# Second expert table: 64 of 256 tokens taken by gathered rows instead of the dense product

## The chip, the cores and the metric

The kernel runs on one core of one Trainium2 chip. The metric is the device time in microseconds of one execution; the value compared is the median of several runs. The engines are TensorE (PE), VectorE (DVE), ScalarE (ACT), GpSimd (POOL) and SyncE (SP), each with an instruction queue of its own.

## The reference, cut to what matters

The program is a first block of two layers (two feed-forward parts around a mixer) and a second block of two layers, each a mixer and an expert part `_peer`. The change touches only the expert part, which runs twice. It has 16384 experts; each of the 256 tokens chooses 128 of them (8 heads of 16), with a softmax gate for each:

```python
    eidx = jnp.take_along_axis(cidx, pos, axis=-1).reshape(T, PEER_HK)
    gate = jax.nn.softmax(sc.astype(jnp.float32), axis=-1).astype(x.dtype).reshape(T, PEER_HK)
...
        ub = jnp.take(u_tab, ib, axis=0)
        act = jax.nn.gelu(jnp.einsum('td,tkd->tk', xb, ub), approximate=False)
        vb = jnp.take(v_tab, ib, axis=0)
        return jnp.einsum('tk,tkd->td', gb * act, vb)
```

The width d is 1024 and everything is float32.

## The kernel before, in words

The expert part does not gather. It computes the activations of all 16384 experts for all 256 tokens, multiplies them by a matrix of gates that is zero where an expert wasn't chosen, and multiplies the result by the whole second table. Both tables come from `in_stream`, 512 KB at a time ("a unit", 128 experts x 1024), through `ring` (three slots, SP's `load`, L497) and are split into two fp32r parts, high and low, in `wsp` (three slots): ACT writes the high part (L454), DVE the low part (L457). A product of two split numbers takes three matmuls, high x high, high x low and low x high (`PARTS`).

**First table (stages U and U2, 92 and 36 units).** Each unit gives 24 matmuls (L721) and one activation. Of each unit's 256 tokens, the columns of the second 128 are written to DRAM (`second_dram`, L518 and L521, SP), to be transposed into the layout that the second table's stage reads. Meanwhile the gates of the first 128 tokens reach the same DRAM tensor by 128 indirect DMAs with addition on POOL (L688, semaphore `scattered`), each of 128 elements. The gates of the second 128 tokens are built in U2 from one-hot matrices in groups of four tokens (`GROUPS` = 32, one group behind each unit from the 94th on): DVE builds four one-hot tiles (L2645, L2654), PE multiplies (L1342, eight matmuls a group), ACT moves them (L1807).

**Second table (stage V, 128 units).** For each unit j: SP fetches `back[j % 4]` from `second_dram` (L527) after waiting for `gated`; DVE multiplies the unit's slice of `arena` by it (`gate`, L2671); ACT writes the high part of the result to `hsp` (`stage`, L1789), DVE the low part (`low`, L2676); PE runs `value_unit` (L1349), which is `down_unit` (L778): two blocks of 128 tokens, each three parts by two halves of 512 columns, 12 matmuls 128x512 (L785), summed over all 128 units in four PSUM banks `ACC`. DVE's order for a unit is gate(j+1), low(j), split of the next unit; ACT's is stage(j), split. The order on each engine is as the code is written; the engines are held together by semaphores alone. POOL has nothing to do in V but fetch `h` and two rows for the layer norm after unit 40 (`RESTORE_AT`, L694). SP issues in V, for each unit, one load of 512 KB and one `back` of 128 KB. After the last unit, DVE adds the four banks to `h` (`add_block`, L1908) and the layer norm follows.

## Time and profile before

| | us |
|---|---|
| median of 3 runs | 2987.77 (2987.75 to 2992.1) |
| the profiled execution | 2988.89 |
| its span in the trace | 2986.9 |
| PE busy in it | 2928.5 |
| DVE busy | 2124.6 |
| ACT busy | 1498.2 |
| POOL busy | 680.0 |

Busy times are sums of instruction durations. Matmuls overlap one another in the pipeline, so their spacing is read from start times. A row of the timeline has the start, the duration, the engine, the line of the kernel, the operation, what it writes and reads, the shape and the count; in square brackets stands the idle time of the engine just before, and what ended it. Stages are told apart by their lines: U2 has L1342, V has L785 with `hsp` and `wsp`.

### The profile page before, as it was taken

Reading aid. Unit: us, or ns where it says so; the run is one execution under the profiler, and the core shown is the slowest. Engines: PE = TensorE matmul, PEld = TensorE weight load, DVE = VectorE, ACT = ScalarE, POOL = GpSimd, SP = SyncE. Lnnn points to the kernel's source line nnn. Section 1 sums busy time; section 2 is a strip of 40 time slices with the busy share of each in tenths; the row PEclk is TensorE's granted clock in tenths of the full one; section 3 lists DMA queues with packets and bytes.
Section 4 is the critical chain, followed back from the end, with each engine's and each line's share of the span. In section 5 each row is a group of like instructions: output and inputs, shape, how many; then the busy total and the mean of one; then the engine's idle time right before and its main releaser. Section 6 shows DMA issues by size and latency. Waiting matters only on the chain.

```text
span 2986.9 us, 54746 instructions
## 1 busy us (share of the span) xinstructions
PE 2928.5 (98%) x18452; PEld 2598.6 (87%) x18452; DVE 2124.6 (71%) x3656; ACT 1498.2 (50%) x2410; POOL 680.0 (23%) x443
## 2 busy tenths in 40 slices
PE   8999999999999999999999999999999999999998
PEld 7888888888878888899999988888899999988887
DVE  6667566766766667758986677777758996767776
...
GB/s 222 190 161 180 153 167 186 174 183 189 148 233 113 184 187 152 157 173 199 198 211 189 176 247 262 243 240 203 163 163 191 196 209 197 176 235 266 239 244 189
DMA packets 255982, 581.52 MB, mean 195 GB/s; under 512 B 61336, under 2 KB 127168, under 8 KB 255344
## 3 DMA queue, kind: packets, MB, share of 16 engines
...
HBM read 542.92 MB, written 36.84 MB: 194 GB/s over the span
## 4 chain that ended last, share of the span: by engine, by line
PE 81%; DVE 10%; ACT 4%; issue 2%; DMA 2%; POOL 1%; SPq 0%; DVEq 0%; ACTq 0%
PE acc L785 31%; PE work L721 26%; PE work L731 9%; PE work L733 5%; DVE wsp L457 4%; PE acc L1205 2%; PE acc L849 2%; ACT wsp L454 2%; DMA ring<-in_stream 2%; PE acc L1342 1%; ACT scratch L1421 1%; PE work L1127 0%; POOL st L584 0%; DVE scratch L2033 0%; PE work L1242 0%
## 5 line engine op out<-in xcount | busy, mean ns | idle before, releaser
L457 DVE TENSOR_TENSOR wsp<-ring,wsp 128x1024 fp32r<-128x1024 f32 x908 | 1105.2, 1225 | 568.7 <-ACT wsp L454 564.4
L454 ACT ACTIVATE wsp<-ring 128x1024 fp32r<-128x1024 f32 x944 | 984.9, 1052 | 506.1 <-PE work L721 251.8
L721 PE MATMUL work<-xsp,wsp 128*128 128x256 f32 x7872 | 971.7, 285 | 6.2 <-DVE wsp L457 3.2
L721 PEld LDWEIGHTS work<-xsp,wsp 128*128 128x128 f32 x7872 | 953.8, 192 | 11.2 <-DVE wsp L457 4.5
L785 PE MATMUL acc<-wsp,hsp 128*128 128x512 f32 x4128 | 955.4, 390 | 6.6 <-DVE hsp L2676 4.7
L785 PEld LDWEIGHTS acc<-wsp,hsp 128*128 128x128 f32 x4128 | 767.8, 188 | 171.1 <-issue 4.4
L731 PE MATMUL work<-xsp,wsp 128*128 128x512 f32 x1408 | 503.7, 400 | 6.5 <-DVE xsp L1861 5.0
L688 POOL DMA_INDIRECT second_dram<-rows_sb,spots x256 | 465.8, 1819 | 148.4 <-issue 90.8
L733 PE MATMUL work<-xsp,wsp 128*128 128x256 f32 x1408 | 395.8, 281 | 0.0
L731 PEld LDWEIGHTS work<-xsp,wsp 128*128 128x128 f32 x1408 | 265.4, 188 | 74.6 <-DVE xsp L1861 6.1
L584 POOL TENSOR_TENSOR st<-st,mhalf 128x1 f32<-128x1 f32 x24 | 20.6, 862 | 1356.4 <-DVE st L1881 805.0
L1789 ACT ACTIVATE hsp<-arena 128x256 fp32r (+1 forms) x256 | 107.0, 418 | 336.4 <-PE acc L785 322.7
L733 PEld LDWEIGHTS work<-xsp,wsp 128*128 128x128 f32 x1408 | 266.7, 189 | 3.1
L2676 DVE TENSOR_TENSOR hsp<-arena,hsp 128x256 fp32r<-128x256 f32 x256 | 108.8, 425 | 60.1 <-ACT hsp L1789 60.0
L1456 ACT ACTIVATE hsp<-scratch 128x256 fp32r<-128x256 f32 x88 | 36.8, 418 | 218.4 <-DVE scratch L1954 218.4
L1448 ACT ACTIVATE scratch<-scratch 128x256 f32<-128x256 f32 x88 | 36.8, 418 | 188.1 <-DVE scratch L1944 188.1
L680 POOL TENSOR_TENSOR wsp<-ring,wsp 128x1024 fp32r<-128x1024 f32 x36 | 89.7, 2492 | 130.6 <-ACT wsp L454 130.4
L2671 DVE TENSOR_TENSOR arena<-arena,back 128x256 f32 (+1 forms) x256 | 107.2, 419 | 10.5 <-ACT arena L1807 6.0
L849 PE MATMUL acc<-wsp,xsp 128*128 128x512 f32 x384 | 100.8, 413 | 0.0
L1205 PE MATMUL acc<-wsp,xsp 128*128 128x512 f32 x384 | 93.9, 397 | 0.0
L849 PEld LDWEIGHTS acc<-wsp,xsp 128*128 128x128 f32 x384 | 72.9, 197 | 16.2
L1205 PEld LDWEIGHTS acc<-wsp,xsp 128*128 128x128 f32 x384 | 70.3, 188 | 15.3
...
## 6 DMA issues: line engine op xcount, KB each, us to landing
...
back<-second_dram SPq DMA_DIRECT2D x256, 128.0 KB, 3.2
...
second_dram<-rows_sb,spots POOLq DMA_INDIRECT x256
...
```

Of the source, the lines that this page charges most:

```text
L454: self.eng.activation(dst[:, 0, :], src, ACT.Copy).then_inc(high_done, 1)
L457: self.eng.tensor_tensor(dst[:, 1, :], src, dst[:, 0, :].bitcast(F32), ALU.subtract)\
L688: pool.indirect_dma_start(out=second_dram[l], in_=selv[:, 0, 2, n:n + 1], in_offset=None, out_offset=bass.IndirectOffsetOnAxis(spots[:, n: ...
L721: mm = pe.matmul(out_, lhsT=w[:, a, 128 * c:128 * c + 128], rhs=xsp[:, b, c, :], start=(c == 0 and n == 0), stop=(c == DC - 1 and n == 2))
L731: pe.matmul(out_, lhsT=w[:, 0, 128 * c:128 * c + 128], rhs=xcs[:, c, :, :].rearrange("p s t -> p (s t)"), start=(c == 0), stop=False)
L733: mm = pe.matmul(out_[:, 0:T], lhsT=w[:, 1, 128 * c:128 * c + 128], rhs=xsp[:, 0, c, :], start=False, stop=(c == DC - 1))
L785: mm = pe.matmul(ACC[2 * b + n][:, :], lhsT=act[:, pa, 128 * b:128 * b + 128], rhs=w[:, pw, 512 * n:512 * n + 512], start=(first and m == ...
L849: mm = pe.matmul(ACC[2 * (g % 2) + b][:, :], lhsT=xsp[:, px, c, 128 * b:128 * b + 128], rhs=w[:, pw, 512 * cc:512 * cc + 512], start=(c == ...
L1205: mm = pe.matmul(ACC[2 * (g % 2) + b][:, :], lhsT=xsp[:, px, c, 128 * b:128 * b + 128], rhs=w[:, pw, 512 * cc:512 * cc + 512], start=(c == ...
L1789: act.activation(hsp[:, j % 2, 0, :], arena[:, bass.ds(it * (6 * T) + j * T, T)], ACT.Copy)\
L2671: tt(a, a, back[j % 4], ALU.mult).then_inc(gated, 1)
L2676: tt(hsp[:, j % 2, 1, :], arena[:, bass.ds(it * (12 * T) + j * T, T)], hsp[:, j % 2, 0, :].bitcast(F32), ALU.subtract).then_inc(act_low, 1)
```

## The change

The second 128 tokens are split into 64 that stay dense (`KEPT`) and 64 that are gathered (`FETCHED`). `arena`, `gate`, `stage`, `low` and `back` shrink from 256 to 192 columns. `GROUPS` falls from 32 to 16.

On PE a value unit has 10 matmuls: the first 128 tokens as before (6), and the 64 kept tokens with their high and low parts interleaved as 128 columns of the stationary side (`gsp`), times the high and the low part of the weights by two halves (4). After the last unit ACT copies these two banks out (`packed`), and PE folds high and low rows together and adds the gathered rows' sum with four float32 matmuls against `fold` (L1485, L1486 of the new kernel).

The 64 gathered tokens have 128 chosen experts each, 8192 rows. They lie on 128 partitions, a token's first eight choices of a head on one, the other eight on the one 64 further. So POOL issues, per layer, 64 indirect DMAs that fetch 128 rows of 4 KB each (`fetch`, 512 KB) into seven slots of `fetched`, and 64 that fetch the 128 activations belonging to them (`fetch_act`, 4 bytes each) from `second_dram`. DVE multiplies activations by gates in four batches of 16 (`coefficients`). Of each seven rows, DVE adds four with one instruction each (`add_row`, 128x1024), and for three (`BY_POOL`) ACT scales the row in place (`scale_row`, 128x1024) and POOL adds it (128x1024). Seven rows are worked into each twelve units ("a round"), from unit 14 to unit 121; nine rounds, and one row more. A slot is fetched anew only when its row has been added, and POOL's queue holds, for each row, its own addition, the fetch for the row seven later, and one or two `fetch_act`. `fetch` for rows 0 to 6 stands before V; POOL then waits for the end of U2, clears the two totals, waits for the last activations to be in DRAM and issues 16 `fetch_act`; the first `coefficients` on DVE waits for those.

Small parts: before the last 16 scatters POOL waits for the second tokens' gates and issues three DMAs that move indices and gates of the upper choices to the lower 64 partitions; every first-table activation is now written in two pieces (L1799 and L1800 before did so in U2 alone), with the second in one of four `acts` slots that is reused once its DMA has landed; POOL's restoring of `h` stands after round 3. The three indirect forms have index lists made on the chip.

On PE, one value unit in the loop before (`wsp` and `hsp` are the split weights and activations):

```order
L1356 UNCONDITIONAL_BRANCH
L1356 ISA
L405 REGISTER_ALU
L785 MATMUL acc<-wsp,hsp 128x512 x12
L1351 REGISTER_ALU
```

and now (`gsp` holds the interleaved parts):

```order
L1475 ISA
L444 REGISTER_ALU
L1460 MATMUL acc<-wsp,gsp 128x512 x4
L1467 MATMUL acc<-wsp,gsp 128x512 x6
L1454 REGISTER_ALU
```

Twelve matmuls of 128x512 became ten, in two statements.

On DVE, inside the loop over the value units, before:

```order
L2669 REGISTER_ALU
L2671 ISA
L2671 TENSOR_TENSOR arena<-arena,back_81 128x256
L2675 REGISTER_ALU
L2676 TENSOR_TENSOR hsp<-arena,hsp 128x256
L456 REGISTER_ALU
L457 TENSOR_TENSOR wsp<-ring,wsp 128x1024
```

and now, from the second unit of a round:

```order
L2852 REGISTER_ALU
L2854 ISA
L2854 TENSOR_TENSOR arena<-arena,back_89 128x192
L2858 REGISTER_ALU
L2859 TENSOR_TENSOR gsp<-arena,gsp 128x192
L502 REGISTER_ALU
L503 TENSOR_TENSOR wsp<-ring,wsp 128x1024
L2736 ISA
L2739 ISA
L2739 SCALAR_TENSOR_TENSOR row_total<-fetched,coef,row_total 128x1024
```

The two short operations are 192 wide, and behind four of the twelve splits there is now an addition of a row, which waits for that row's DMA.

On POOL, from the scatters to the end of V, before (all of it):

```order
L676 COMPARE_AND_BRANCH
L688 DMA second_dram<-rows_sb,spots 4194304x1 x128
L694 DMA h<-h_saved_dram 128x2048
L614 DMA rows_sb<-in_rows 128x1024
L615 DMA rows_sb<-in_rows 128x1024
```

and now, its beginning up to the third row of the first round:

```order
L763 DMA second_dram<-rows_sb,spots 4194304x1 x112
L756 DMA gidx<-gidx 64x8x8 x2
L757 DMA fgate<-fgate 64x8x8
L763 DMA second_dram<-rows_sb,spots 4194304x1 x16
L742 DMA fetched<-in_stream,gidx 128x1024 x7
L770 MEMSET row_total 128x1024
L771 MEMSET row_total_62 128x1024
L748 DMA coef<-second_dram,gidx 128x1 x16
L742 DMA fetched<-in_stream,gidx 128x1024
L748 DMA coef<-second_dram,gidx 128x1 x2
L786 TENSOR_TENSOR row_total_62<-row_total_62,fetched 128x1024
```

After 128 scatters POOL had three DMAs; now there are 128 indirect DMAs and 28 additions, each in a queue whose next instruction waits for it.

The diff, cut:

```diff
-GROUPS = P // 4
+FETCHED = 64
+TD = T - FETCHED
+KEPT = TD - P
...
+HALF_K = TOPK // 2
+ROWS = PH * HALF_K
+SLOTS = 7
+ROUNDS = ROWS // SLOTS
+BY_POOL = (1, 3, 5)
+BATCH = 16
+BATCHES = ROWS // BATCH
+SEGMENTS = ((0, 2, 1), (2, 4, 2), (4, 6, 3), (6, 9, 4))
+ROW_AT = (1, 2, 4, 6, 7, 9, 11)
+USES = [len(range(s, ROWS, SLOTS)) for s in range(SLOTS)]
 ROUND = 16 * TOPK
...
+                sp.dma_start(second_rows[l][bass.ds(it * UNITS_BODY + j, 1)][:, :, P:T].rearrange("a p t -> p (a t)"),
+                             acts[:, j % 4, :]).then_inc(acts_slot[j % 4], 16)
...
+                sp.dma_start(back[j % 4][:, 0:TD], second_rows[l][bass.ds(it * UNITS_BODY + j, 1)][:, :, 0:TD].rearrange("a p t -> p (a t)"))\
                   .then_inc(back_in[j % 4], 16)
...
+                def fetch(m):
+                    r, k = m % SLOTS, place_of(m)
+                    if m >= SLOTS:
+                        if r in BY_POOL:
+                            pool.wait_ge(used_pool, by_pool(ROWS) * l + by_pool(m - SLOTS + 1))
+                        else:
+                            pool.wait_ge(used_dve, by_dve(ROWS) * l + by_dve(m - SLOTS + 1))
+                    pool.indirect_dma_start(out=fetched[:, r, :], out_offset=None, in_=value_rows,
+                                            in_offset=bass.IndirectOffsetOnAxis(gidx[:, 0, k:k + 1], 0))\
+                        .then_inc(row_in[r], 16)
+
+                def fetch_act(m):
+                    k = place_of(m)
+                    pool.indirect_dma_start(out=coef[:, m:m + 1], out_offset=None, in_=second_dram[l],
+                                            in_offset=bass.IndirectOffsetOnAxis(gidx[:, 1, k:k + 1], 0))\
+                        .then_inc(elem_in[m // BATCH], 16)
...
+                    if i == PH - 1:
+                        pool.wait_ge(ev("sel_ready"), 3 * (l + 1))
+                        for w in range(2):
+                            pool.dma_start(low_halves(gidx[0:64, w, :]), high_halves(gidx[64:P, w, :])).then_inc(rows_moved, 16)
+                        pool.dma_start(low_halves(fgate[0:64, :]), high_halves(fgate[64:P, :])).then_inc(gates_moved, 16)
...
+                pool.wait_ge(rows_moved, 32 * (l + 1))
+                for m in range(SLOTS):
+                    fetch(m)
+                pool.wait_ge(unit_done, Group(f"peer{l}", "V").u)
+                pool.memset(row_total, 0.0)
+                pool.memset(row_total2, 0.0).then_inc(totals_clear, 1)
                 for s in range(4):
...
+                    pool.wait_ge(acts_slot[s], 16 * SPILLS * (l + 1))
+                for m in range(BATCH):
+                    fetch_act(m)
+                more = BATCH
+                for t in range(ROUNDS):
+                    for r in range(SLOTS):
+                        m = SLOTS * t + r
+                        if r in BY_POOL:
+                            n = by_pool(ROWS) * l + by_pool(m)
+                            pool.wait_ge(row_scaled, n + 1)
+                            pool.wait_ge(totals_clear, l + 1)
+                            if n:
+                                pool.wait_ge(used_pool, n)
+                            pool.tensor_tensor(row_total2, row_total2, fetched[:, r, :], ALU.add).then_inc(used_pool, 1)
+                        if m + SLOTS < ROWS:
+                            fetch(m + SLOTS)
+                        while more < min(ROWS, BATCH + (4 * m + 6) // 3):
+                            fetch_act(more)
+                            more += 1
+                    if t == 3:
+                        pool.wait_ge(scattered, ROUND * PH * (l + 1))
+                        pool.wait_ge(g_done, GROUPS * (l + 1))
+                        pool.wait_ge(gated, NKEYS * l + RESTORE_AT)
+                        pool.dma_start(h, saved).then_inc(h_back, 16)
+                        load_rows(rows2[2 * l + 2, 0], rows2[2 * l + 2, 1])
+                pool.wait_ge(used_dve, by_dve(ROWS) * (l + 1))
+                pool.wait_ge(used_pool, by_pool(ROWS) * (l + 1))
+                pool.tensor_tensor(row_total, row_total, row_total2, ALU.add).then_inc(ev("rows_added"), 1)
                 serve(pool, moments[:, 0, 1:2])
                 serve(pool, moments[:, 1, 1:2])
...
-                    down_unit(G, i, hsp[:, i % 2, :, :], first, last, 6 * n)
+                    w = G.unit(pe, i, 6 * n)
+                    both = gsp[:, i % 2, :, :].rearrange("p t s -> p (t s)")
+                    act = gsp[:, i % 2, :, :]
+                    for m in range(2):
+                        for n in range(2):
+                            mm = pe.matmul(ACC[2 + n][:, :], lhsT=both[:, 2 * P:2 * TD], rhs=w[:, m, 512 * n:512 * n + 512],
+                                           start=(first and m == 0), stop=(last and m == 1))
+                    if last:
+                        mm.then_inc(ev("packed_done"), 1)
+                    order = [(m, n) for n in range(2) for m in range(3)] if last else [(m, n) for m in range(3) for n in range(2)]
+                    for m, n in order:
+                        pa, pw = PARTS[m]
+                        mm = pe.matmul(ACC[n][:, :], lhsT=act[:, 0:P, pa], rhs=w[:, pw, 512 * n:512 * n + 512],
+                                       start=(first and m == 0), stop=(last and m == 2))
+                        if last and m == 2 and n == 0:
+                            mm.then_inc(ev("half_block"), 1)
+                    mm.then_inc(unit_done, 1)
...
+                pe.wait_ge(ev("rows_added"), l + 1)
+                for n in range(2):
+                    pe.wait_ge(packed_out, 2 * l + n + 1)
+                    c = slice(512 * n, 512 * n + 512)
+                    pe.matmul(ACC[2 + n][:, :], lhsT=fold[:, 64:192], rhs=row_total[:, c], start=True, stop=False)
+                    mm = pe.matmul(ACC[2 + n][:, :], lhsT=fold[:, 0:P], rhs=packed[:, c], start=False, stop=True)
+                    mm.then_inc(ev("first_block" if n else "half_block"), 1)
...
+                    if q >= 4:
+                        act.wait_ge(acts_slot[q % 4], 16 * (SPILLS * l + q // 4) + (4 * UNITS_BODY) * it)
+                    act.activation(arena[:, bass.ds(it * (UNITS_BODY * TD) + q * TD, P)], G.bank(q)[:, 0:P], ACT.Gelu)
+                    G.free(act.activation(acts[:, q % 4, :], G.bank(q)[:, P:T], ACT.Gelu), q)
...
+                    act.activation(gsp[:, j % 2, :, 0], arena[:, bass.ds(it * (12 * TD) + j * TD, TD)], ACT.Copy)\
                        .then_inc(act_high, 1)
+
+                def scale_row(m, it=0):
+
+                    r = m % SLOTS
+                    act.wait_ge(row_in[r], 16 * (USES[r] * l + m // SLOTS + 1) + 16 * it)
+                    act.activation(fetched[:, r, :], fetched[:, r, :], ACT.Copy, scale=coef[:, bass.ds(it * SLOTS + m, 1)])\
+                       .then_inc(row_scaled, 1)
...
+                for first, last, batches in SEGMENTS:
+                    act.wait_ge(ev("coef_ready"), BATCHES * l + batches)
+                    with act.Fori(0, last - first) as it:
+                        for j in range(12):
+                            k = 14 + 12 * first + j
+                            stage(k, it)
+                            split.one(G.u + k + 1, it, 12)
+                            if j in ROW_AT and ROW_AT.index(j) in BY_POOL:
+                                scale_row(SLOTS * first + ROW_AT.index(j), it)
...
+                    m = slice(BATCH * b, BATCH * (b + 1))
+                    if b == 0:
+                        dve.wait_ge(gates_moved, 16 * (l + 1))
+                    dve.wait_ge(elem_in[b], 16 * BATCH * (l + 1))
+                    c = coef[:, m].rearrange("p (h k) -> p h k", k=HALF_K)
+                    heads = BATCH // HALF_K
+                    g = fgate.rearrange("p (h k) -> p h k", k=TOPK)[:, heads * b:heads * (b + 1), 0:HALF_K]
+                    step(tt(c, c, g, ALU.mult))
+                    dve.memset(st[:, 31:32], 0.0).then_inc(ev("coef_ready"), 1)
...
+                def add_row(m, it=0):
+
+                    r = m % SLOTS
+                    n = by_dve(ROWS) * l + by_dve(m)
+                    per_round = SLOTS - len(BY_POOL)
+                    dve.wait_ge(row_in[r], 16 * (USES[r] * l + m // SLOTS + 1) + 16 * it)
+                    if n:
+                        dve.wait_ge(used_dve, n + per_round * it)
+                    stt(row_total, fetched[:, r, :], coef[:, bass.ds(it * SLOTS + m, 1)], row_total, ALU.mult, ALU.add)\
+                        .then_inc(used_dve, 1)
...
+                    a = arena[:, bass.ds(it * (12 * TD) + j * TD, TD)]
+                    tt(a, a, back[j % 4][:, 0:TD], ALU.mult).then_inc(gated, 1)
...
+                    tt(gsp[:, j % 2, :, 1], arena[:, bass.ds(it * (12 * TD) + j * TD, TD)],
+                       gsp[:, j % 2, :, 0].bitcast(F32), ALU.subtract).then_inc(act_low, 1)
...
+                dve.wait_ge(totals_clear, l + 1)
+                for first, last, batches in SEGMENTS:
+                    coefficients(batches - 1)
+                    with dve.Fori(0, last - first) as it:
+                        for j in range(12):
+                            k = 14 + 12 * first + j
+                            gate(k + 1, it)
+                            low(k, it)
+                            split.one(V.u + k + 1, it, 12)
+                            if j in ROW_AT and ROW_AT.index(j) not in BY_POOL:
+                                add_row(SLOTS * first + ROW_AT.index(j), it)
                 split.next = V.u + 123
+                add_row(ROWS - 1)
```

## Rows read from the trace of the kernel before

**Rows 1.** Page, parts 1 and 5: busy time of PE; POOL's indirect scatter and its split.
```profile
PE 2928.5 (98%) x18452; PEld 2598.6 (87%) x18452; DVE 2124.6 (71%) x3656; ACT 1498.2 (50%) x2410; POOL 680.0 (23%) x443
...
L688 POOL DMA_INDIRECT second_dram<-rows_sb,spots x256 | 465.8, 1819 | 148.4 <-issue 90.8
...
L680 POOL TENSOR_TENSOR wsp<-ring,wsp 128x1024 fp32r<-128x1024 f32 x36 | 89.7, 2492 | 130.6 <-ACT wsp L454 130.4
```

**Rows 2.** Windows: stretch, length, busy by engine, clock, DMA share, GB/s; U2, then V.
```profile
1600.00:1710.00 110.00, 110.00 (x1035) 108.67 (x1033) 80.51 (x154) 61.34 (x131) 68.00 (x39) 1.00 0.75 181
1720.00:2060.00 340.00, 337.30 (x1485) 278.55 (x1486) 245.91 (x374) 170.37 (x249) 1.73 (x3) 1.00 0.75 246
```

**Rows 3.** Timeline of V, DVE rows of one unit (layer 1).
```profile
1802.30 1.23 DVE L457 TENSOR_TENSOR wsp<-ring,wsp 128x1024 fp32r<-128x1024 f32 x1 [0.52 <-ACT wsp L454]
1803.44 0.42 DVE L2671 TENSOR_TENSOR arena<-arena,back 128x256 f32 x1
...
1805.01 1.23 DVE L457 TENSOR_TENSOR wsp<-ring,wsp 128x1024 fp32r<-128x1024 f32 x1 [0.53 <-ACT wsp L454]
```

**Rows 4.** Timeline of PE: first and last matmuls around V; units of U2.
```profile
1714.19 2.00 PE L785 MATMUL acc<-wsp,hsp 128*128 128x512 f32 x8
...
2066.20 4.70 PE L743 MATMUL work<-xsp 128*128 128x512 f32 x20
...
2610.15 0.63 PE L1342 MATMUL acc<-one_hots 128*128 128x128 f16 x8
2610.59 3.12 PE L721 MATMUL work<-xsp,wsp 128*128 128x256 f32 x24
2613.55 0.63 PE L1342 MATMUL acc<-one_hots 128*128 128x128 f16 x8
...
2617.39 8.88 PE L721 MATMUL work<-xsp,wsp 128*128 128x256 f32 x72
2626.11 4.27 PE L785 MATMUL acc<-wsp,hsp 128*128 128x512 f32 x18
```

**Rows 5.** Line L688: duration ns min/median/max.
```profile
L688 POOL DMA_INDIRECT second_dram<-rows_sb,spots x256: 1537/1581/2631, 1390.3 to 2595.1; - x128
```

**Rows 6.** Timeline of POOL and DVE in U: scatters beside splits.
```profile
1577.69 2.58 POOL L688 DMA_INDIRECT second_dram<-rows_sb,spots  x1 [0.30 <-issue]
1580.57 2.58 POOL L688 DMA_INDIRECT second_dram<-rows_sb,spots  x1 [0.30 <-issue]
...
1577.62 1.23 DVE L457 TENSOR_TENSOR wsp<-ring,wsp 128x1024 fp32r<-128x1024 f32 x1 [1.66 <-ACT wsp L454]
```

**Rows 7.** Timeline of POOL and DVE in U: casts beside POOL's addition.
```profile
1355.53 2.40 POOL L680 TENSOR_TENSOR wsp<-ring,wsp 128x1024 fp32r<-128x1024 f32 x1 [0.47 <-ACT wsp L454]
...
1355.70 2.28 DVE L2519 CAST pfa<-posa 128x64 f16<-128x64 uint32 x1
1358.02 0.20 DVE L2520 CAST pfb<-posi 128x64 f16<-128x64 uint32 x1
```

**Rows 8.** Timeline, POOL and SP: a wait for scatters; the last scatter; SP's reads after it.
```profile
1653.08 2.21 POOL L688 DMA_INDIRECT second_dram<-rows_sb,spots  x1 [4.59 <-DMA second_dram<-rows_sb,spots]
...
1689.59 1.63 POOL L688 DMA_INDIRECT second_dram<-rows_sb,spots  x1 [0.30 <-issue]
...
1701.74 0.36 SPq L527 DMA_DIRECT2D back<-second_dram  x1
...
1718.28 0.80 SPq L527 DMA_DIRECT2D back<-second_dram  x2
```

**Rows 9.** Windows in V while h and two rows also came (columns as Rows 2).
```profile
1828.00:1832.00 4.00, 2.68 (x12) 1.88 (x10) 1.90 (x3) 1.60 (x3) 0.00 (x0) 1.00 0.91 360
2736.00:2740.00 4.00, 4.00 (x19) 3.30 (x19) 1.47 (x3) 0.62 (x2) 0.00 (x0) 1.00 1.00 361
```

**Rows 10.** Windows of the first mixer: PE idle, then the clock.
```profile
290.00:292.00 2.00, 0.11 (x1) 0.00 (x0) 0.80 (x1) 2.00 (x5) 2.00 (x4) 1.00 0.98 358
294.00:296.00 2.00, 2.00 (x16) 1.88 (x15) 0.83 (x3) 0.24 (x1) 0.00 (x0) 0.50 1.02 268
```

153 lines of the change are left out of this document (95 added, 58 removed).

## The prediction

> **What bounds the kernel now.** I read the page first: PE is busy 2928.5 us, 98% of the span [rows 1]. The windows then show it in both stages that the change touches: 110.00 of 110 us in U2, 337.30 of 340 in V, at full clock, while DVE is at 246 and ACT at 170 of those 340 and POOL does next to nothing [rows 2]. So in V the matmuls set the pace. From the start of one split to the next are 1805.01 - 1802.30 = 2.71 us [rows 3], 0.226 for each of 12 matmuls. V lasts 2066.20 - 1714.19 = 352 us a layer [rows 4], 128 units and 5 us of start. Everything here is made against the profiled execution, 2988.9 us with 2986.9 of span, 1.1 over the median.
>
> **What PE gains.** Ten matmuls in place of twelve are 2.26 us a unit, 128 x 2.26 = 289 us a layer. If nothing else changed, V would be 58 us shorter. In U2 a unit with a one-hot group takes 2613.55 - 2610.15 = 3.40 us, one without 8.72/3 = 2.91 (2617.39 to 2626.11) [rows 4]; sixteen groups less are 16 x 0.49 = 7.8 us a layer. PE is full there, so I count them whole. I price the stationary side read with a gap at nothing; double would make it the bound, and that is counted below.
>
> **What POOL must now do in V.** This is the term that decides. An indirect DMA holds POOL for 1.82 us on the mean of 256 and 0.30 passes before the next can start: 2.12 [rows 1, 6]. The smallest is 1.54 [rows 5], so 1.84. The large ones come from DVE: the scatter at 1577.69 starts 0.07 after a split and takes 2.58, which is what is left of the split (1.16) plus 1.42; the next one meets the next split and takes 2.58 again, 2.88 a turn [rows 6]. No trace here shows an indirect DMA that fetches 4 KB rows. Each issue handles 128 indices as the scatter does, so I take the scatters' 2.12, with 1.84 and 2.88 as ends. An addition of 128x1024 on POOL is 2.49 us [rows 1]; with its wait for DVE's port 2.75.
>
> The Trainium skill, SBUF — State Buffer (Who interferes with whom), says that a DVE instruction with two SBUF inputs and a GpSimd instruction that reads SBUF exclude one another for a whole instruction. The trace shows the lock in both directions: beside POOL's addition a cast of 0.20 us took 2.28, ending with it [rows 7], and the scatters above waited for the split. By that page all of DVE's V work contends.
>
> For a round of twelve units POOL has 7 fetches, 9.3 fetches of activations while these last, and three additions: 16.3 x 2.12 + 3 x 2.75 = 42.9 us. PE's twelve units take 27.1. For the time of PE a fetch would have to cost (27.1 - 8.25)/16.3 = 1.15 us, below anything the trace shows. **So POOL sets the pace** until the last activation has been asked for, behind row 35. Row m+7 can't be fetched before POOL comes by in its queue, and DVE, which has gate, low and split of the next units queued behind the row's addition, waits there; PE waits for DVE. Seven slots let DVE be one round ahead and no more.
>
> In order of time, from the first matmul of V:
> - 5 us: POOL clears two totals and waits for the last activations in DRAM; SP's reads behind the same wait went at 1718.28, 4.1 us after V's start [rows 4, 8]. In the first layer POOL comes from its row fetches: the last scatter was issued at 1691.2 [rows 8], the three copies (3 us) and 7 x 2.12 bring it to 1709, and V now starts at 1706; that hides in the 5.
> - 16 x 2.12 = 34 us for the first activations, 4 to land (a wait for scatters ended 4.59 us after the last [rows 8]), and 6 for DVE's two units and first addition: 49. DVE is there after 14 units, at 32 us, so PE stands for some 12 us.
> - Rows 0 to 35: 36 + 48 = 84 indirect DMAs, 178.1 us; 15 additions, 41.3; restoring h, three short issues, 2: 221. That is 270.
> - Row 42 lands and DVE takes up unit 86: 4 + 2, 276.
> - 42 units remain. POOL needs only 7 x 2.12 + 8.25 = 23 us a round now. But DVE has a round's 12 x (1.14 + 2 x 0.27) + 4 x 1.2 = 25 us (1803.44 - 1802.30 for a split, the gate's spacing less 64 columns [rows 3]), and the three additions of POOL can stop it for 3 x 2.3 more: 32. And the DMA engines: 524 + 98 KB a unit and 7/12 of 524 for rows are 928 KB, at 360 GB/s [rows 9] 2.57 us. Between PE's 2.26 and DVE's 2.66 I take 2.5 for 36 units and 2.26 for six: 104. That is 380.
> - The tail: two evictions and four float32 matmuls behind the last unit. Four matmuls at 0.226 would be 0.9, at four times that 3.6, since these are plain float32; I take 2.5, an estimate. POOL's last addition hides in the six last units.
>
> V is then 382, 30 more than before. The three copies ahead of the last 16 scatters push these back by about 3 us, while SP comes to them 7.8 us earlier; SP's first read stood 10.5 us behind the last scatter's end (1701.74 against 1691.2), so up to 3 us of waiting arise there: 1.5. Per layer 30 - 7.8 + 1.5 = 24, for two 47: 2988.9 + 47 = 3036, and I say **3035**.
>
> What costs nothing: the second activation of each U unit (ACT is busy 170 of 340 in V, and 61 of 110 in U2, where it already does two [rows 2]); the four index operations of DVE before V; the slots of `acts`, reused after four units, 11 us, against a landing of a few; ACT's three scalings a round, in an engine with half its time free.
>
> The Trainium skill, DMA: Bandwidth & Descriptors (Specifications), gives about 358 GB/s of HBM for a core; by it the late rounds would take 2.59 us a unit. The rows show the same figure.
>
> **Rivals.**
> - *POOL is cheaper.* Fetches run at 1.84 and DVE isn't held up: 5 + 29.4 + 10 for the start, 84 x 1.84 + 15 x 2.49 + 2 = 194, then 6 + 42 x 2.26 + 2.5 = 103: V is 342. With 7.8 and 1.5 that is 16 less a layer, 2956. With my other terms the kernel breaks even at V = 358, which is 170 + 100 x, x = 1.88 a fetch. That is near, and so the sign hangs on a quarter of a microsecond. For it: 1.58 is the median of the scatters [rows 5], and DVE, while it waits for rows, doesn't hold the port. Against: the mean was 1.82 with DVE no fuller than in the new V.
> - *The change gives all of PE's gain.* V is 289 + 7, and the sum 2 x (56 + 7.8) less: 2862. It needs fetches of 1.15 us.
> - *POOL is dearer*, by locking step with the splits at 2.88 as in [rows 6], or because a fetch of 4 KB rows costs more to describe. V = 170 + 288 = 458, 100 more a layer: 3189. Half way is 3110.
> - *The clock.* After PE had been busy 0.11 of 2 us, its granted clock was 0.50 (1.2 GHz instead of 2.4) for the next microseconds [rows 10]. While POOL sets the pace, a row takes 6.1 us and PE works 12/7 x 2.26 = 3.9 of it. At half clock this would be 7.7, above 6.1, and if it lasted for all 36 rows it would cost 58 us a layer: 3150. Since PE works two thirds of that time, I expect it for a part only, hidden in the waits. The gapped stationary side lies here too: at double load time (0.376 for each of ten) a unit is 3.8 us.
> - *It doesn't do what it says*: the order of the instructions shows ten matmuls and 16 groups, so only the tail could be other than said, by microseconds.
>
> **How the numbers follow.** The forecast (POOL sets the pace of five rounds, fetches between 1.95 and 2.35, late rounds between 2.26 and 2.66; 3000 to 3085) gets 0.47. The cheaper POOL, 2940 to 3000, 0.27; the whole gain 0.05; the dearer POOL and the clock 0.19; 0.02 for what I don't see. Leaving out the whole gain and the top of the dearer case, the range is 2945 to 3125. A measurement of this kernel tells 0.2%, 6 us, from no change. Of the cheaper case nine tenths lie below 2982: faster 0.30, same 0.07, slower 0.63.
>
> **What would show it.** In the profile of the changed kernel: POOL's two indirect forms back to back from V's start, with a mean near 1.8 us and 0.3 between; a PE stretch idle for some 10 us about 32 us into V; in the first two thirds of V, DVE's additions of rows waiting for DMAs whose issue waited in POOL's queue, PE busy about 65%, and DMA below 300 GB/s; then a last third with PE nearly full, a unit in 2.4 to 2.7 us and DMA near 350 GB/s; U2 8 us shorter. The forecast is wrong if fetches take 1.5 us or less between starts, if the rows' landings and not POOL's queue hold DVE, or if PE is the one that is full throughout V.

## The result and the profile after

The changed kernel took 3050.65 us (3038.73 to 3056.78, 4 runs) against 2988.16 (2987.75 to 2992.1, 4 runs) for the kernel before: a ratio of 1.0203, 95% interval 1.0178 to 1.0227. It is slower, by about 2%, inside the range and 16 us above the predicted 3035. The profiled execution of it was one of 3056.78 us, so its trace stands some 6 us above the median.

The page of the changed kernel, parts 1 and 5 (columns as in the rows of before):

```profile
span 3054.9 us, 53849 instructions
...
PE 2879.0 (94%) x17700; PEld 2517.0 (82%) x17700; DVE 2233.0 (73%) x3634; ACT 1539.7 (50%) x2616; POOL 1194.6 (39%) x765
...
L763 POOL DMA_INDIRECT second_dram<-rows_sb,spots x256 | 496.0, 1937 | 127.2 <-issue 80.7
...
L742 POOL DMA_INDIRECT fetched<-in_stream,gidx x128 | 183.5, 1434 | 157.0 <-DVE row_total L2739 132.1
...
L748 POOL DMA_INDIRECT coef<-second_dram,gidx x128 | 155.8, 1218 | 52.8 <-issue 38.4
...
L786 POOL TENSOR_TENSOR row_total<-row_total,fetched 128x1024 f32<-128x1024 f32 x54 | 132.6, 2456 | 55.7 <-ACT fetched L1929 55.1
```

PE has fallen from 98% busy [rows 1] to 94%: it is no longer full. The new rows say at once that the fetches are cheap. Their means of 1.43 and 1.22 us are below the 1.94 us of the scatters in the same trace, and in front of the row fetches POOL was idle for 132 us, waiting for DVE's additions.

The timeline of PE, from the end of U2 to the matmuls with `fold`, first layer 0, then layer 1. U2's matmuls are L824, a unit of V is L1460 and L1467, the matmuls with `fold` are L1485 and L1486:

```profile
1705.35 4.60 PE L824 MATMUL work<-xsp,wsp 128*128 128x256 f32 x24 [1.99 <-DVE wsp L503]
1709.79 1.09 PE L1460 MATMUL acc<-wsp,gsp 128*128 128x512 f32 x4
...
2086.35 1.08 PE L1460 MATMUL acc<-wsp,gsp 128*128 128x512 f32 x4
2087.26 1.56 PE L1467 MATMUL acc<-wsp,gsp 128*128 128x512 f32 x6
2088.66 1.08 PE L1460 MATMUL acc<-wsp,gsp 128*128 128x512 f32 x4
...
2093.29 1.02 PE L1485 MATMUL acc<-row_total,fold 128*128 128x512 f32 x2
...
2096.32 4.01 PE L846 MATMUL work<-xsp 128*128 128x512 f32 x15
```
```profile
2646.10 3.11 PE L824 MATMUL work<-xsp,wsp 128*128 128x256 f32 x24 [2.02 <-DVE wsp L503]
2651.35 1.93 PE L1460 MATMUL acc<-wsp,gsp 128*128 128x512 f32 x4 [2.14 <-issue]
...
3041.49 1.02 PE L1486 MATMUL acc<-fetched,fold 128*128 128x512 f32 x2
```

V begins at 1709.79 instead of 1714.19 [rows 4], 4.4 us sooner, and its next stage at 2096.32 instead of 2066.20. So V took 386.5 us where it had taken 352.0, and layer 0 costs 30.1 us. In layer 1, V runs from 2651.35 to 3042.5, 391.2 us; the kernel before started it at 2626.11 [rows 4] and was through some 351 us later. The 68.0 us between the two spans are + 34.5 (V, layer 0), + 40 (V, layer 1), - 4.4 and - 4.9 (U2), and 3 behind the last V. A unit that nothing holds takes 2088.66 - 2086.35 = 2.31 us; 128 of them would be 296. With the 3 us of `fold` that is 299. The loss against that is 87 us in layer 0 and 92 in layer 1, and it is made within V.

Windows of V in layer 0 (stretch, length, busy by engine, granted clock, DMA share, GB/s): the first 38 us, the stretch behind it, and one in the last third:

```profile
1720.00:1748.00 28.00, 27.59 (x120) 22.46 (x118) 22.16 (x41) 15.63 (x24) 17.65 (x15) 1.00 0.83 266
1748.00:1964.00 216.00, 180.61 (x696) 138.29 (x694) 186.52 (x236) 111.72 (x157) 166.21 (x109) 0.94 0.87 304
1964.00:2020.00 56.00, 47.01 (x178) 36.35 (x177) 47.85 (x64) 28.96 (x41) 24.80 (x16) 0.91 0.90 301
```

Waits of the same V, 1712 to 2093 us (engine, what it was to do, what ended the wait; us in all, times, longest), and DVE's additions of rows (count | busy us, mean ns | idle us before them):

```profile
ACT gsp L1922 <- PE acc L1467: 82.2, 72, 3.8
PEld acc L1460 <- issue: 67.8, 48, 3.9
POOL fetched L742 <- DVE row_total L2739: 64.3, 22, 9.4
PE acc L1460 <- DVE gsp L2859: 57.3, 44, 3.5
ACT wsp L500 <- DMA ring<-in_stream: 52.2, 43, 3.7
```
```profile
L2739 DVE SCALAR_TENSOR_TENSOR row_total<-fetched,coef,row_total 128x1024 f32<-128x1024 f32 x37 | 47.2, 1276 | 0.1
```

Up to 1748 PE is full. From then on, to 1964, four things are near full together, and none quite: DVE 86%, the DMA engines 87%, PE 84%, and POOL 77%, or 87% with the 0.3 us that pass after each of its indirect DMAs. PE waits 57 us for `low` (L2859) on DVE, ACT waits 52 us for the transfers of the dense table. POOL, which was to set the pace, waits 64 us for DVE, while DVE in front of its 37 additions of rows stood for 0.1 us in all: no row came late.

### The profile page after: what moved, and what is told of

Same layout as the page of the kernel before. It is cut to its first block, busy times and chain, and to the rows that moved or that the text cites. A ratio compares the mean times of both kernels' runs of the same rounds, so it can differ in the third digit from the quotient of the medians.

```text
span 3054.9 us, 53849 instructions
## 1 busy us (share of the span) xinstructions
PE 2879.0 (94%) x17700; PEld 2517.0 (82%) x17700; DVE 2233.0 (73%) x3634; ACT 1539.7 (50%) x2616; POOL 1194.6 (39%) x765
## 4 chain that ended last, share of the span: by engine, by line
PE 41%; POOL 16%; DVE 14%; issue 12%; DMA 10%; ACT 7%; DVEq 1%; ACTq 0%; SPq 0%; POOLq 0%
POOL second_dram L763 15%; PE work L824 9%; PE acc L888 7%; DMA ring<-in_stream 7%; PE work L834 7%; DVE wsp L503 5%; ACT wsp L500 5%; PE work L836 3%; PE acc L1467 3%; PE acc L952 3%; PE acc L1308 2%; PE acc L1460 2%; DMA second_dram<-rows_sb,spots 2%; DVE row_total L2739 1%; DVE gsp L2859 1%
## 5 line engine op out<-in xcount | busy, mean ns | idle before, releaser
L824 PE MATMUL work<-xsp,wsp 128*128 128x256 f32 x7872 | 964.1, 284 | 7.8 <-DVE wsp L503 4.9
L824 PEld LDWEIGHTS work<-xsp,wsp 128*128 128x128 f32 x7872 | 951.9, 192 | 12.9 <-issue 6.3
L763 POOL DMA_INDIRECT second_dram<-rows_sb,spots x256 | 496.0, 1937 | 127.2 <-issue 80.7
L1467 PE MATMUL acc<-wsp,gsp 128*128 128x512 f32 x1536 | 419.3, 409 | 0.0
L1460 PE MATMUL acc<-wsp,gsp 128*128 128x512 f32 x1024 | 303.7, 420 | 117.5 <-DVE gsp L2859 114.9
L1467 PEld LDWEIGHTS acc<-wsp,gsp 128*128 128x128 f32 x1536 | 311.7, 203 | 66.4
L1460 PEld LDWEIGHTS acc<-wsp,gsp 128*128 128x128 f32 x1024 | 193.5, 198 | 201.3 <-issue 136.0
L888 PE MATMUL acc<-wsp,hsp 128*128 128x512 f32 x1056 | 256.8, 392 | 1.7 <-DVE hsp L2109 1.7
L742 POOL DMA_INDIRECT fetched<-in_stream,gidx x128 | 183.5, 1434 | 157.0 <-DVE row_total L2739 132.1
L1922 ACT ACTIVATE gsp<-arena 128x192 fp32r (+1 forms) x256 | 96.9, 379 | 264.5 <-PE acc L1467 165.9
L888 PEld LDWEIGHTS acc<-wsp,hsp 128*128 128x128 f32 x1056 | 191.9, 188 | 44.1 <-DVE hsp L2109 3.4
L748 POOL DMA_INDIRECT coef<-second_dram,gidx x128 | 155.8, 1218 | 52.8 <-issue 38.4
L2854 DVE TENSOR_TENSOR arena<-arena,back 128x192 f32 (+1 forms) x256 | 153.9, 601 | 22.8 <-DMA back<-second_dram 20.9
L786 POOL TENSOR_TENSOR row_total<-row_total,fetched 128x1024 f32<-128x1024 f32 x54 | 132.6, 2456 | 55.7 <-ACT fetched L1929 55.1
```

The source lines that it names most:

```text
L742: pool.indirect_dma_start(out=fetched[:, r, :], out_offset=None, in_=value_rows, in_offset=bass.IndirectOffsetOnAxis(gidx[:, 0, k:k + 1], 0))\
L748: pool.indirect_dma_start(out=coef[:, m:m + 1], out_offset=None, in_=second_dram[l], in_offset=bass.IndirectOffsetOnAxis(gidx[:, 1, k:k + ...
L763: pool.indirect_dma_start(out=second_dram[l], in_=selv[:, 0, 2, n:n + 1], in_offset=None, out_offset=bass.IndirectOffsetOnAxis(spots[:, n: ...
L824: mm = pe.matmul(out_, lhsT=w[:, a, 128 * c:128 * c + 128], rhs=xsp[:, b, c, :], start=(c == 0 and n == 0), stop=(c == DC - 1 and n == 2))
L888: mm = pe.matmul(ACC[2 * b + n][:, :], lhsT=act[:, pa, 128 * b:128 * b + 128], rhs=w[:, pw, 512 * n:512 * n + 512], start=(first and m == ...
L1460: mm = pe.matmul(ACC[2 + n][:, :], lhsT=both[:, 2 * P:2 * TD], rhs=w[:, m, 512 * n:512 * n + 512], start=(first and m == 0), stop=(last an ...
```

## Experiments

All experiments start from the changed kernel. What they are compared by is the length of V in the profile, from its first matmul to the first matmul with `fold` (3 us before V's end). It is 383.5 and 387.6 us in the two layers of the changed kernel, 386 on the mean. A time without an interval is that of one execution. The four executions of the changed kernel lie 18 us apart, 9 a layer, and the profiled one is the slowest of them, 3 us a layer over the median; a difference to its 386 us that is not well above 9 us is not shown by one execution. The kernel before took 2987.84 us beside the first four kernels below (dense part, short rows, memsets, all by DVE), 2994.11 beside the next four (short rows with memsets, short rows all by DVE, transfers alone, additions alone) and 2991.86 beside the other three (half width, row work alone, activations fetched twice).

### The dense part alone

```diff
-                for m in range(SLOTS):
-                    fetch(m)
...
-                            if j in ROW_AT and ROW_AT.index(j) not in BY_POOL:
-                                add_row(SLOTS * first + ROW_AT.index(j), it)
```
(likewise without `fetch_act`, `coefficients`, `scale_row` and POOL's additions)

> Left out: all indirect fetches of rows and activations, their scaling and additions (ACT, DVE, POOL); the gathered sum is zero, so the 64 tokens get no expert output. The ten matmuls, the fold and the rest stay. Measures the dense part alone. In the changed kernel an undisturbed value unit takes 2.31 us (last units of V), so V should be 128 x 2.31 + 8 = 304 us instead of 386, and the time 3051 - 2 x 82 = 2887, if all of the loss comes from the gathered rows. Were the interleaved stationary side, the split activations or the tail slow by themselves, V would stay above 320 and the time above 2920.

Measured: 2892.11 us; V 302.8 and 307.3, 305 on the mean. Windows:

```profile
1748.00:1964.00 216.00, 212.55 (x916) 174.08 (x915) 163.91 (x275) 124.17 (x183) 4.11 (x4) 1.00 0.85 273
```

PE is full at full clock with the gapped stationary side, so that rival is dead: ten matmuls a unit do give nearly what they were counted at. The 80.5 us that V is longer in the changed kernel are the 64 gathered tokens. But look at the rest of the row: DMA share 0.85, DVE 76%. There was little room beside it.

### Take away one cost from the whole

Three kernels, each with one part of the gathered work lightened. Short rows: after a layer's first seven, rows are fetched 64 columns wide.

```diff
-                    pool.indirect_dma_start(out=fetched[:, r, :], out_offset=None, in_=value_rows,
+                    width, source = (D, value_rows) if m < SLOTS else (64, stream.rearrange("n p (a d) -> (n p a) d", d=64))
+                    pool.indirect_dma_start(out=fetched[:, r, 0:width], out_offset=None, in_=source,
```

> Rows 7 to 63 are fetched 64 columns wide (256 bytes, from other places of the stream) instead of 1024; every instruction and wait stays, only 94% of the rows' bytes go, and the sums are wrong. Three theories. Lock (POOL's additions shut DVE out, 3 x 2.4 us a round): little gain, V stays above 345 us, time above 2965. Transfers (DMA engines full, the stream late): V falls to about 315, time 2910. Queue (POOL's queue paces the rows, the theory of the prediction): V stays 380 to 390, time 3045.

Measured: 3033.94 us; V 370.6 and 374.1. The queue's range and that of the transfers are both missed; only the lock's bound (V above 345 us) holds.

Memsets in place of POOL's additions:

```diff
-                            pool.tensor_tensor(row_total2, row_total2, fetched[:, r, :], ALU.add).then_inc(used_pool, 1)
+                            step(pool.memset(row_total2, 0.0))
+                            step(pool.memset(row_total2, 0.0))
+                            pool.memset(row_total2[:, 0:512], 0.0).then_inc(used_pool, 1)
```

> POOL's addition of a row is replaced by three memsets of together about the same length (2.4 us), which write only and read nothing, so POOL's rows are missing from the sum. POOL stays as busy, the transfers stay the same. Lock: DVE is no longer shut out, V falls by 30 us or more a layer, time 2985 or less. Transfers: within 15 us of 3051. Queue: unchanged, 3045 to 3055.

Measured: 3040.55 us; V 375.0 and 376.3. The lock's forecast, 2985 us or less, is missed, and so is that of the queue (3045 to 3055); that of the transfers (within 15 us of 3051) is met. The time lies among the four of the changed kernel (3038.73 to 3056.78), so this gain isn't clear of the noise.

All additions by DVE (ACT then scales no row either):

```diff
-BY_POOL = (1, 3, 5)
+BY_POOL = ()
```

> All seven rows of a round are added by DVE; ACT scales none and POOL adds none (BY_POOL empty). Same result, same transfers. Lock: DVE has 12 x 1.68 + 7 x 1.2 = 28.6 us a round instead of 25.0 plus up to 7 of waiting, so a round falls from about 35 to 30 us and the time to about 2960, below the kernel before. Transfers alone: no gain, 3040 or more. Queue: POOL loses 8 us a round, time about 2970 as well, so this run doesn't tell lock from queue but shows whether there is a version that wins.

Measured: 3022.27 us (3013.71 to 3026.11), a ratio of 1.0109 to the kernel before, interval 1.0085 to 1.0132; V 366.7 and 366.8. It computes everything, and is the better of the two complete versions: 19 us a layer less in V than the changed kernel by the two profiles, 14 a layer by the two medians, still slower than before. All forecasts are missed, 2960 to 2970 us for lock and queue and 3040 for the transfers. Its window has the DMA engines as the fullest of all:

```profile
1748.00:1964.00 216.00, 185.75 (x740) 143.41 (x740) 179.45 (x270) 101.92 (x149) 110.18 (x93) 0.97 0.93 323
```

Each cost, taken away alone, gives back 10 to 19 us of 80 by the profiles, and of these only the 19 come from more than one execution. From these three it looked as if either of two causes, bytes or lock, were enough for nearly the whole loss. The next kernels tested that.

### Take away two

Short rows and memsets together:

> Edit: both earlier edits at once. After the first 7 fetches of a layer each value row is fetched as 64 columns instead of 1024 (from 4 KB to 256 B a partition), and GpSimd's 27 additions a layer are each three memsets of the total that take about as long. Left out: the rest of each fetched row, and GpSimd's part of the value sums; the queue, the counts of fetches and all waits stay. Either edit alone left the value stage at 371 to 375 us where the dense part alone needs 303. Theory A (two holders, each sufficient by itself: the bytes, and the additions of GpSimd that stop VectorE): with both away the stage falls to 305 to 320 us and the run to 2893 to 2925 us. Theory B (a third holder: GpSimd's queue of 128 indirect transfers a layer, or VectorE and ScalarE being full with the 64 rows): it stays above 340 us a layer and the run above 2965 us.

Measured: 2964.1 us; V 343.2 and 337.3, 340 on the mean. Theory A missed: 35 us are left with the bytes and the lock gone, at the edge of what theory B asked for. Some of them are POOL's queue after all. The timeline of DVE and PE:

```profile
1810.67 1.28 DVE L2742 SCALAR_TENSOR_TENSOR row_total<-fetched,coef,row_total 128x1024 f32<-128x1024 f32 x1
1820.34 0.17 DVE L2731 TENSOR_TENSOR coef<-coef,fgate 128x16 f32<-128x16 f32 x1 [8.39 <-DMA coef<-second_dram,gidx]
...
1822.01 2.07 PE L1463 MATMUL acc<-wsp,gsp 128*128 128x512 f32 x4 [9.32 <-DVE gsp L2862]
```

DVE came 8.4 us too early for a batch of 16 activations, and PE stood for 9.3 us. In the changed kernel DVE waits for no batch in either layer.

Short rows, all added by DVE:

> Edit: VectorE adds all 64 rows of a layer (none by GpSimd), and after the first 7 each fetched row is 64 columns wide, so that the bytes are nearly gone. Left out: the rest of each row in the value sums. The kernel in which VectorE adds all the rows with full bytes has a stage of 367 us. Theory A (there the bytes hold it): the stage falls to 315 to 330 us, where VectorE with 12 units at about 1.94 us and 7 rows at 1.22 us (31.8 us) is the slower against TensorE's 27.7 us a round, so 9.1 rounds at up to 31.8 us are the upper bound, 290 us, plus the 12 units before and some 20 behind the rounds: the run at 2915 to 2945 us. Theory B (VectorE's own occupancy and its hand-overs with ScalarE hold it, not the bytes): it stays at 350 to 367 us, the run at 2985 to 3020 us.

Measured: 2963.57 us; V 340.0 and 341.0. Neither: 26 us less than with full rows, so the bytes did hold that kernel, but 35 us more than the dense part, 10 above the top of what A gave.

### One cost alone, on top of the dense part

If two causes together can't be told apart by removing them, they can by adding each alone. The transfers of the rows alone, released by DVE's `gate` of the unit in question (likewise without the fetches of activations, `coefficients`, `scale_row` and all additions):

```diff
+                            pool.wait_ge(gated, NKEYS * l + 14 + 12 * t + ROW_AT[r] + 2)
                             fetch(m + SLOTS)
```

> Edit: the dense part with 192 tokens, and of the other 64 tokens only the fetches of the value rows, at full width, each released by the unit at which its addition would have stood. Left out: the fetches of the activations, the scaling and every addition of a row. Theory A (the bytes alone can hold the stage): 64 transfers of 512 KB beside 128 pairs of the dense table, 113 MB by the count of the copies, at the 304 to 323 GB/s that the changed kernel and the one with all additions on VectorE moved, are 350 to 372 us: the stage lands at 345 to 367 us. Theory B (transfers hold it only together with the additions on VectorE, which delay the release of buffers): the stage stays within 303 to 325 us, and the moved bytes go over 350 GB/s. Run: 2975 to 3020 us by A, 2890 to 2935 us by B.

Measured: 2978.53 us; V 345.2 and 348.4, 347 on the mean. Window and the two largest waits behind POOL's own:

```profile
1748.00:1964.00 216.00, 194.62 (x792) 148.63 (x790) 138.17 (x236) 107.43 (x159) 52.49 (x49) 0.99 0.97 345
```
```profile
ACT wsp L500 <- DMA ring<-in_stream: 114.1, 87, 5.4
DVE wsp L503 <- ACT wsp L500: 89.8, 80, 6.1
```

Theory A held. With nobody adding a row, the bytes alone cost 42 us, at a DMA share of 0.97: ACT waits for the dense table, DVE for ACT, PE for DVE. This is also near the floor of the whole idea in this form. With every row moved and none added, V is 347 us and the 3 us of `fold` behind it, against some 351.5 of the kernel before.

The same at half the width:

```diff
-                    pool.indirect_dma_start(out=fetched[:, r, :], out_offset=None, in_=value_rows,
+                    width, source = (D, value_rows) if m < SLOTS else (512, stream.rearrange("n p (a d) -> (n p a) d", d=512))
+                    pool.indirect_dma_start(out=fetched[:, r, 0:width], out_offset=None, in_=source,
```

> Edit: as the kernel with the transfers alone (stage 345 to 349 us), but each fetch behind the first 7 brings 512 columns instead of 1024, so half the bytes with the same number of transfers. Left out besides: half of each row. Theory A (the rate of the transfers is the limit: there 345 GB/s at a DMA share of 0.97): 64 fetches of 256 KB less 7 full ones and the dense pairs are about 98 MB, 285 us at 345 GB/s, under the 303 us of the dense part, so the stage falls to 303 to 315 us and the run to 2892 to 2920 us. Theory B (each fetch costs the stage something fixed, by its descriptors or its place among the others, and not by its bytes): the stage keeps at least half of the 42 us, 325 us or more, and the run 2935 us or more.

Measured: 2932.56 us; V 322.9 and 323.3, 323. Window:

```profile
1748.00:1964.00 216.00, 206.30 (x860) 163.18 (x860) 150.00 (x256) 117.78 (x172) 57.85 (x54) 0.99 0.93 316
```

With about half the bytes 18 us of the 42 remain. Neither theory: A gave up to 10, B 20 or more, which is missed by 2. The fetched bytes are 57 x 0.26 + 7 x 0.52 = 18.6 MB instead of 33.5, 55%, and the cost 43%. So it goes about with the bytes, and it is there at a share of 0.93 already. That a ring transfer lands later when it shares the engines with a row's, and that the chain behind it has little in hand, is what ACT's waits for the ring suggest: 88.4 us in this kernel from 1712 to 2000, 114.1 with full rows.

POOL's additions alone:

```diff
+                        pool.wait_ge(gated, NKEYS * l + 14 + 12 * t + ROW_AT[r] + 2)
+                        pool.wait_ge(row_in[r], 16 * (l + 1))
...
+                        pool.tensor_tensor(row_total2, row_total2, fetched[:, r, :], ALU.add).then_inc(used_pool, 1)
```

> Edit: the dense part with 192 tokens, and of the other 64 tokens only GpSimd's 27 additions a layer of 128x1024 float32, each released by the unit at which it would stand. Left out: the fetches behind the first 7 rows, the fetches of the activations, the scaling and VectorE's additions. Theory A (an addition of GpSimd stops VectorE for its whole 2.4 us, and TensorE with it, whatever slack VectorE has): 27 x 2.3 = 62 us, a stage of 350 to 367 us and a run of 2985 to 3020 us. Theory B (VectorE takes the stop from its slack: 12 units at 1.94 us, 23.3 us, beside TensorE's 27.7 us leave 4.4 us a round against 3 x 2.3 = 6.9 us): 2.5 us a round, 23 us a layer, a stage of 315 to 335 us and a run of 2915 to 2955 us.

Measured: 2943.49 us; V 329.9 and 331.7, 331 on the mean: theory B. Window, and POOL and DVE in it:

```profile
1748.00:1964.00 216.00, 201.93 (x840) 159.96 (x839) 181.63 (x252) 113.52 (x168) 52.90 (x24) 0.99 0.79 251
```
```profile
1850.46 2.46 POOL L783 TENSOR_TENSOR row_total<-row_total,fetched 128x1024 f32<-128x1024 f32 x1 [7.40 <-DVE arena L2844]
...
1851.21 2.78 DVE L503 TENSOR_TENSOR wsp<-ring,wsp 128x1024 fp32r<-128x1024 f32 x1 [0.57 <-ACT wsp L500]
```

The split that meets an addition ends 1.07 us behind it (1853.99 against 1852.92), nearly as if it had begun when POOL was done (1.22 us is its usual time). DVE makes up part of it; 26 us a layer stay, 0.95 for each of 27 additions.

The work of DVE and ACT on the rows alone (37 additions, 27 scalings a layer, no fetches):

```diff
-                    dve.wait_ge(elem_in[b], 16 * BATCH * (l + 1))
...
+                        step(dve.memset(coef, 0.0))
...
-                    dve.wait_ge(row_in[r], 16 * (USES[r] * l + m // SLOTS + 1) + 16 * it)
+                    dve.wait_ge(row_in[r], 16 * (l + 1))
```

> Edit: the dense part with 192 tokens, and of the other 64 tokens only VectorE's 37 additions a layer and ScalarE's 27 scalings, at their places, on the first 7 fetched rows and with coefficients of zero. Left out: the fetches behind the first 7 rows, the fetches of the activations, GpSimd's additions. Theory A (the occupancy of VectorE and ScalarE is what is left in the kernel with short rows and memsets, 338 to 343 us: VectorE has 1.23 + 2 x 0.35 us for a unit and 1.28 us for a row, 2.34 us with 37 rows over 116 units, beside TensorE's 2.31 us, and the two wait for each other in turn): a stage of 330 to 343 us and a run of 2945 to 2970 us. Theory B (what is left there is GpSimd's queue, the late first batch of activations and the short transfers): a stage of 303 to 315 us and a run of 2892 to 2915 us.

Measured: 2944.88 us; V 328.1 and 327.6, 2 us under the range of A and 13 over that of B. Occupancy of the two engines alone is 23 us. By subtraction, the other 12 that are left in the kernel with short rows and memsets are POOL's queue and the short transfers; that the costs add in this way is not shown.

```profile
1748.00:1964.00 216.00, 206.35 (x859) 163.17 (x859) 182.68 (x295) 136.53 (x193) 1.71 (x3) 0.99 0.80 257
```

### More work for POOL's queue

```diff
                             fetch_act(more)
+                            pool.indirect_dma_start(out=spare[:, more:more + 1], out_offset=None, in_=second_dram[l],
+                                                    in_offset=bass.IndirectOffsetOnAxis(gidx[:, 1, place_of(more):place_of(more) + 1], 0))\
+                                .then_inc(spare_in, 16)
                             more += 1
```

> Edit: each of the 48 activation fetches that GpSimd issues between its additions is issued twice, the second into a spare column; nothing is left out. Theory A (as predicted, GpSimd's queue paces the first two thirds of the value stage): every further indirect transfer there lengthens the stage by its whole cost, 48 x 1.4 = 67 us a layer at the 1.09 us and the 0.3 us of issue measured in the changed kernel, 48 x 2.12 = 102 us at the predicted price: a run of 3180 to 3255 us. Theory B (GpSimd's queue has slack, since in the changed kernel it waited 64 us for VectorE and 28 us for ScalarE in the stage): at most 10 us a layer, a run of 3045 to 3070 us.

Measured: 3115.12 us; V 419.0 and 410.3, 29 us a layer over the changed kernel. It lies between the theories. The added transfers took 1.20 us each on the mean and 0.30 of issue, 72 us a layer. Some 43 of it did not lengthen V, and 29 came through. POOL's two waits, for DVE in front of fetches and for ACT in front of additions, fell from 64 and 28 us to 31 and 24 in layer 0, which is most of the 43. How, two rows of PE and DVE's wait show:

```profile
1835.57 2.07 PE L1467 MATMUL acc<-wsp,gsp 128*128 128x512 f32 x4 [23.54 <-DVE gsp L2866]
1917.82 2.07 PE L1467 MATMUL acc<-wsp,gsp 128*128 128x512 f32 x4 [16.52 <-DVE gsp L2866]
```
```profile
DVE coef L2735 <- DMA coef<-second_dram,gidx: 36.2, 3, 19.4
```

This is the stall of the prediction, at the batches of activations, in a kernel whose queue is long enough. In the changed kernel there is no such wait.

## Why the prediction was right in its number and wrong in its mechanism

V over the dense part alone, per layer (mean of both):

| kernel | V, us | over 305 |
|---|---|---|
| row transfers alone | 347 | 42 |
| the same at half width | 323 | 18 |
| POOL's additions alone | 331 | 26 |
| row work of DVE and ACT alone | 328 | 23 |
| short rows and memsets | 340 | 35 |
| short rows, DVE adds all | 340 | 35 |
| full rows, DVE adds all | 367 | 62 |
| short rows | 372 | 67 |
| memsets | 376 | 71 |
| the changed kernel | 386 | 81 |
| the changed kernel, later activations fetched twice | 415 | 110 |

Three costs alone are 42 + 26 + 23 = 91, together 81, and the 91 leave out POOL's queue of fetches of activations. So there is no one cause. The table also shows how the two largest work together. With short rows and memsets 35 us are left; POOL's additions on top of that make 67 (32 more), the full bytes 71 (36 more), but both only 81 (46 more, not 68; 43 at the median of the changed kernel). So each costs about as much beside the row work as alone, and beside one another they share some 22 us, as they would if both stopped the same units. That would explain why removing one of them from the whole gives back so little: 10 us for the lock and 13 for the bytes, both near the noise of one execution.

Point by point:

- **PE's gain: right.** 2.26 us a unit was predicted, 2.31 measured; the dense part alone is 305 us for 296 predicted with its start. Whether the 0.05 us a unit, 6 us a layer, come from the stationary side was not taken apart.
- **The price of an indirect DMA: the step that failed.** "I take the scatters' 2.12, with 1.84 and 2.88 as ends." The trace of the changed kernel has, for the two lines (duration ns min/median/max):

```profile
L742 POOL DMA_INDIRECT fetched<-in_stream,gidx x128: 933/1088/4164, 1698.9 to 2992.0; - x128
```
```profile
L748 POOL DMA_INDIRECT coef<-second_dram,gidx x128: 941/1097/3097, 1717.5 to 2886.1; - x128
```

  1.09 + 0.30 = 1.4 us at the median, and 1.6 on the mean (1.43 and 1.22 us on the page, and 0.30), both below the lower end. The gather is not the accumulating scatter of [rows 5], whose smallest was 1.54; they share a name in the profile and 128 indices. It was a bound with no reason that excluded less.
- **POOL sets the pace: wrong.** A round was priced at 42.9 us. At the median it is 16.3 x 1.4 + 3 x 2.75 = 31 us, near PE's 27; on the mean, with what DVE holds up, it is 34, and twelve units took 37 between 1748 and 1964 (69.6 units in 216 us). POOL is nearly full there, but it is POOL that waits for DVE's additions, and DVE never for a row. Here its queue after the first batch:

```profile
1740.83 1.10 POOL L748 DMA_INDIRECT coef<-second_dram,gidx  x1 [0.30 <-issue]
1751.34 4.16 POOL L742 DMA_INDIRECT fetched<-in_stream,gidx  x1 [9.41 <-DVE row_total L2739]
```

  The 16 activations had been asked for by 1742, 32 us into V, and DVE met the first `coefficients` at 1744.98 without a wait. The 12 us stall of PE there did not come; the row of the window 1720 to 1748 has PE at 27.59 of 28. PE busy at 65% and DMA below 300 GB/s were to show the pace of POOL's queue; the window behind has 84% and 304. The prediction's own mark for a wrong forecast, 1.5 us or less between the starts of fetches, is met by the median (1.4) and not by the mean (1.6). By the formula beside the first rival, 170 + 100 x, a fetch of 1.4 us gives V = 310 and a kernel 3% faster, one of 1.6 us V = 330 and a kernel 2% faster. So the deciding term came out on the other side of its break-even (1.88), and the kernel was slower all the same: what the rival of the cheaper POOL left out were the costs of a full chain, bytes, locks and occupancy, which the sum had only for the last 42 units.
- **The late rounds: mis-sized, for the same reason.** 2.5 us a unit was taken, and 2.94 measured (123.5/42). DVE at 2.66 and DMA at 2.57 stood beside it, each as a bound by itself. Both hold up units in turn, and not in the last rounds alone. The matmuls of L1460 (four a unit) show it, in the first 260 us of V and in the rest:

```profile
1709.70:1969.80 260.10, 101.96 (x344) 64.84 (x344) 0.95 0.87 304
1969.80:2093.30 123.50, 49.36 (x168) 31.91 (x168) 0.96 0.83 281
```

  The first 260 us saw 344/4 = 86 units, where the prediction had needed 276; the last 42 took 123.5 us, where it had 104, both without the tail. The two errors are - 16 and + 20, and that is how 382 stood against 386.5: the number was right by luck, two errors cancelling.
- **The lock: right as a mechanism, under-weighted.** The prediction had three stops of 2.3 us a round. In the changed kernel:

```profile
1866.63 4.04 DVE L503 TENSOR_TENSOR wsp<-ring,wsp 128x1024 fp32r<-128x1024 f32 x1 [1.27 <-ACT wsp L500]
...
1867.17 2.40 POOL L786 TENSOR_TENSOR row_total<-row_total,fetched 128x1024 f32<-128x1024 f32 x1
...
1871.33 1.19 PE L1460 MATMUL acc<-wsp,gsp 128*128 128x512 f32 x4 [2.45 <-DVE gsp L2859]
```

  The split takes 4.04 instead of 1.22 us, ends 1.10 behind POOL's addition, and PE stands for 2.45. It is what [rows 7] showed, now in V. The Trainium skill, SBUF — State Buffer (Who interferes with whom), has the rule that a DVE instruction with two SBUF inputs contends with a GpSimd instruction that reads SBUF; the trace agrees. The price of the lock here is 26 us a layer alone, 32 beside the row work, and 10 on top of all the rest.
- **DMA at 360 GB/s [rows 9]: a price from too short a stretch.** Those are windows of 4 us. Over 216 us the transfers alone reached 345 GB/s, and then PE already lost 42 us a layer. 113 MB a layer at 345 is 328 us, and 347 was measured; a stage that must not wait for its table can't be planned at the peak.
- **U2 and SP's wait: 7.8 - 1.5 = 6.3 predicted, 4.4 and 4.9 measured.** A unit with a one-hot group is as before; PE then waits at the end of U2, 1.99 us in layer 0 and 2.02 + 2.14 in layer 1. SP's rows have the likely reason in layer 0: it came to the read behind the scatters early and stood there from 1695 to 1700, with the ring's next transfer behind it.

```profile
1694.66 0.43 SPq L563 DMA_DIRECT2D second_dram<-acts  x1
1700.11 0.80 SPq L570 DMA_DIRECT2D back<-second_dram  x2
1700.96 0.43 SPq L546 DMA_DIRECT2D ring<-in_stream  x1
```

- **The tail: 2.5 predicted, 3.03 measured** (2093.29 to 2096.32). Each of the four float32 matmuls with `fold` stands in the trace as two records 0.43 us apart, so it takes 0.86, 3.8 times the 0.226 of the others: about the "four times" under which the 2.5 was taken.
- **The clock** fell in stretches where PE had waited, and the windows above have 0.94 and 0.91: after a wait of 3.24 us four matmuls took 2.07 us instead of 1.08, at a granted clock of 0.50, the level of 1.2 GHz.

```profile
1884.65 2.07 PE L1460 MATMUL acc<-wsp,gsp 128*128 128x512 f32 x4 [3.24 <-DVE gsp L2859]
```
```profile
1884.60:1886.70 2.10, 2.05 (x5) 1.67 (x6) 2.10 (x4) 2.10 (x3) 1.57 (x2) 0.50 0.96 385
```

  It is no small matter. Over V of layer 0, in the changed kernel and in the dense part alone, PE's 1280 matmuls of the units and the clock were:

```profile
1709.80:2093.30 383.50, 325.92 (x1283) 251.82 (x1282) 327.65 (x431) 200.34 (x286) 236.11 (x154) 0.95 0.86 296
```
```profile
1706.90:2009.70 302.80, 297.98 (x1282) 243.86 (x1281) 228.69 (x386) 174.47 (x259) 5.96 (x6) 1.00 0.84 271
```

  The same matmuls kept PE busy 28 us longer, and it stood idle 53 us longer; together these are the 81. Some of the 28 may lie where PE would have waited anyway. The clock is no cause of its own here, since it fell behind waits, but it may make each of the other costs larger; no run takes it away.

What stays open: what the clock adds, and how much of the 12 us between row work alone and short rows with memsets is the queue and how much the short transfers. Each cost alone is from one profiled execution with its two layers, which agree within 6 us everywhere but in the last line of the table (8.7).
